# FFN activations of an encoder kernel kept in class order; the up products read them in token order

## The reference, cut to what matters

```python
h = rms_norm(x, ffn_pre_norm[l])
x = x + rms_norm(conv_gated_mlp(h, w_up[l], ffn_conv[l], w_down[l]), ffn_post_norm[l])

def conv_gated_mlp(h, w_up, conv_w, w_down):
    S = h.shape[1]
    u = h @ w_up                                   # 256 x 1024 by 1024 x 5632
    pad = CONV_WIDTH // 2
    up = jnp.pad(u, ((0, 0), (pad, pad), (0, 0)))
    u = sum(up[:, t:t + S] * conv_w[t] for t in range(CONV_WIDTH))
    gate, val = jnp.split(u, 2, axis=-1)
    return (jax.nn.gelu(gate, approximate=True) * val) @ w_down
```

## Time and profile before

| | |
|---|---|
| median of 3 runs | 1053.47 us (1053.18 to 1053.96) |
| the profiled execution | 1052.44 us |
| its span, first to last instruction | 1050.5 us |
| PE (matmuls) busy | 1026.9 us, 98% |
| PEld (weight loads) busy | 919.9 us, 88% |
| DVE busy | 657.0 us, 63% |
| ACT busy | 586.4 us, 56% |
| POOL busy | 127.0 us, 12% |
| mean granted clock of TensorE | 0.999 of full speed |
| read from HBM | 168.72 MB, 162 GB/s over the span |

### The profile page before, as it was taken

How to read it: one execution, slowest core, us unless ns; L and a number is a source line. 1 busy time by engine, 2 the same in 40 slices (tenths; PEclk the granted TensorE clock), 3 DMA queues, 4 the chain that set the end, 5 groups by cost and what they waited for, 6 DMA issues and landing times.

```text
span 1050.5 us, 15947 instructions
## 1 busy us (share of the span) xinstructions
PE 1026.9 (98%) x6325; PEld 919.9 (88%) x6325; DVE 657.0 (63%) x866; ACT 586.4 (56%) x843; POOL 127.0 (12%) x233
## 2 busy tenths in 40 slices
PE   7899999999999999999999999999999999999997
PEld 6789989888877999999898899998888789999996
DVE  4635566555585876767674345666555867676765
ACT  4567665555536554554475666665653466455452
POOL 3452133000000000000014421230000000000000
PEclk9999999999999999999999999999999999999999
DMA  8554445544434555555355543464345535555541
GB/s 233 176 169 141 123 149 164 178 161 160 141 130 171 169 186 207 179 182 201 119 180 173 150 142 120 130 222 160 122 154 179 167 128 175 200 193 168 201 160 41
DMA packets 106189, 170.79 MB, mean 163 GB/s; under 512 B 3345, under 2 KB 72772, under 8 KB 106116
## 3 DMA queue, kind: packets, MB, share of 16 engines
q1 hardware_dynamic: 104684, 166.36, 48.0%
q10 hardware_dynamic: 1352, 3.16, 0.9%
q0 software_dynamic: 80, 0.26, 0.2%
HBM read 168.72 MB, written 1.05 MB: 162 GB/s over the span
## 4 chain that ended last, share of the span: by engine, by line
PE 88%; DVE 5%; ACT 2%; DVEq 2%; DMA 1%; issue 1%; POOL 0%; POOLq 0%; ACTq 0%; SPq 0%
PE bank L1268 26%; PE bank L1270 26%; PE bank L1269 25%; PE bank L1558 2%; PE bank L1465 1%; PE bank L1486 1%; DVEq L1126 1%; PE bank L1551 1%; DVE hT_lo L996 1%; DVE merged L1127 1%; DVE w_lo L975 1%; PE bank L1474 1%; PE bank L1502 1%; DMA w_raw<-in_w_in_dram 1%; DMA par_rows<-in_attn_pre_norm_dram 1%
## 5 line engine op out<-in xcount | busy, mean ns | idle before, releaser
L975 DVE TENSOR_TENSOR w_lo<-w_raw,w_hi 128x2048 fp32r<-128x2048 f32 (+3 forms) x174 | 363.0, 2098 | 192.8 <-ACT w_hi L647 192.8
L647 ACT ACTIVATE w_hi<-w_raw 128x2048 fp32r<-128x2048 f32 (+3 forms) x174 | 302.4, 1752 | 52.3 <-PE bank L1270 46.7
L1268 PE MATMUL bank<-w_hi,hT_lo 128*128 128x512 f32 (+2 forms) x700 | 258.5, 369 | 2.8 <-DVE w_lo L975 2.7
L1270 PE MATMUL bank<-w_hi,hT_hi 128*128 128x512 f32 (+2 forms) x700 | 253.0, 361 | 0.0
L1269 PE MATMUL bank<-w_lo,hT_hi 128*128 128x512 f32 (+2 forms) x700 | 252.5, 361 | 0.0
L1268 PE MATMUL bank<-hT_hi,w_lo 128*128 128x256 f32 x704 | 199.9, 284 | 3.5 <-DVE hT_lo L996 3.2
L1269 PE MATMUL bank<-hT_lo,w_hi 128*128 128x256 f32 x704 | 199.2, 283 | 0.0
L1270 PE MATMUL bank<-hT_hi,w_hi 128*128 128x256 f32 x704 | 199.2, 283 | 0.0
L1268 PEld LDWEIGHTS bank<-w_hi,hT_lo 128*128 128x128 f32 x700 | 131.5, 188 | 19.3 <-DVE w_lo L975 3.8
L1270 PEld LDWEIGHTS bank<-w_hi,hT_hi 128*128 128x128 f32 x700 | 131.4, 188 | 14.1
L1269 PEld LDWEIGHTS bank<-w_lo,hT_hi 128*128 128x128 f32 x700 | 131.7, 188 | 13.1
(11 more groups left out here) (203 smaller groups left out, 1247.4 us busy)
## 6 DMA issues: line engine op xcount, KB each, us to landing
w_raw<-in_w_up_dram SPq DMA_DIRECT2D x44, 1024.0 KB, 4.9
w_raw<-in_w_in_dram SPq DMA_DIRECT2D x36, 1024.0 KB, 5.0
w_raw<-in_w_in_dram SPq DMA_DIRECT2D x36, 768.0 KB, 4.3
w_raw<-in_w_down_dram SPq DMA_DIRECT2D x22, 1024.0 KB, 5.4
w_raw<-in_w_out_dram SPq DMA_DIRECT2D x8, 1024.0 KB, 4.9
w_raw<-in_w_in_dram SPq DMA_DIRECT2D x8, 672.0 KB, 4.9
w_raw<-in_w_branch_mla_dram SPq DMA_DIRECT2D x4, 1024.0 KB, 4.8
w_raw<-in_w_branch_diff_dram SPq DMA_DIRECT2D x4, 1024.0 KB, 5.0
```

Of the source, the lines that this page charges most:

```text
L647: nc.scalar.activation(w_hi[:, n % RING, 0:nk * cols], raw[:, n % RING, 0:nk * cols], ACT.Copy).then_inc(hi_done, 1)
L975: V.tensor_tensor(w_lo[:, n % RING, s], raw[:, n % RING, s], w_hi[:, n % RING, s].bitcast(F32), ALU.subtract).then_inc(lo_done, 1)
L1268: PE.matmul(dst, lhs[1], rhs_hi, start=start, stop=False)
L1270: return PE.matmul(dst, lhs[0], rhs_hi, start=False, stop=stop)
```

## The change

The copies of the FFN turn no longer reorder: ACT and DVE write `hT_hi` and `hT_lo` contiguously, in class order, as in the other turns. The reordering goes into the read of the moving operand. A new view, `token_order`, walks place 64r + j with r innermost, so that the 256 columns come as 64 groups of 4 words, each word 64 words from the last. The PSUM view of the output is written with the same two dimensions but is contiguous, as before. The results in the banks, the convolution, `g` and the down products are the same. The number of instructions, all waits and all DMAs stay.

```diff
--- before.py
+++ after.py
@@ -449,13 +449,9 @@
             nk, cols = PIECES[n][3:5]
             return buf[:, n % RING, 0:nk * cols].rearrange("p (k n) -> p k n", k=nk)
 
-        def own_order(cols):
-
-            return cols.rearrange("p (j r) -> p r j", r=4)
-
-        def by_class(cols):
-
-            return cols.rearrange("p (r j) -> p r j", r=4)
+        def token_order(cols):
+
+            return cols.rearrange("p (r j) -> p j r", r=4)
 
         def own_order2(cols):
             return cols.rearrange("p (c j r) -> p c r j", c=2, r=4)
@@ -748,8 +744,6 @@
                         g0 = {"attn": PRE_A, "ffn": PRE_F, "latent": G_Q}[what]
                         for k in range(nk):
                             col, from_bank = dst[:, k0 + k, :], src[:, k * SEQ:(k + 1) * SEQ]
-                            if what == "ffn":
-                                col, from_bank = own_order(col), by_class(from_bank)
                             last = nc.scalar.activation(col, from_bank, ACT.Copy,
                                                         scale=par_all[:, l, g0 + k0 + k:g0 + k0 + k + 1])
                     last.then_inc(turn_hi, 1)
@@ -991,8 +985,6 @@
                         g0 = {"attn": PRE_A, "ffn": PRE_F, "latent": G_Q}[what]
                         for k in range(nk):
                             lo_k, hi_k, from_bank = lo[:, k0 + k, :], hi[:, k0 + k, :].bitcast(F32), src[:, k * SEQ:(k + 1) * SEQ]
-                            if what == "ffn":
-                                lo_k, hi_k, from_bank = own_order(lo_k), own_order(hi_k), by_class(from_bank)
                             last = V.scalar_tensor_tensor(out=lo_k, in0=from_bank, scalar=par_all[:, l, g0 + k0 + k:g0 + k0 + k + 1],
                                                           in1=hi_k, op0=ALU.mult, op1=ALU.subtract)
                     last.then_inc(turn_emptied, 1)
@@ -1342,9 +1334,9 @@
                         for k in range(8):
                             if j == 0:
                                 wait_turned(l, kind, c, k)
-                            last = passes(bank[4 + c % 4][:, j * SEQ:(j + 1) * SEQ],
+                            last = passes(bank[4 + c % 4][:, j * SEQ:(j + 1) * SEQ].rearrange("p (q r) -> p q r", r=4),
                                           (hi[:, k, j * P:(j + 1) * P], lo[:, k, j * P:(j + 1) * P]),
-                                          hT_hi[:, k, :], hT_lo[:, k, :], k == 0, k == 7)
+                                          token_order(hT_hi[:, k, :]), token_order(hT_lo[:, k, :]), k == 0, k == 7)
                     last.then_inc(piece_used, 1)
                     return
                 halves = 2 if cols == 1024 else 1
```

## The result

The changed kernel takes 1087.01 us (median of 4 runs, 1086.35 to 1088.54), the kernel before 1053.72 us beside it. The ratio is 1.0321, 95% interval 1.0306 to 1.0337: 33.3 us slower. The forecast was 1725 us with 1265 as the lower end. The sign was right, the size far out.

What follows compares the result with a forecast made beforehand. The prediction took PE, busy 98% of the span, as the bound: 675.8 us more for the up products' strided read, less 4.3 for the copies, on 1053.5 gave 1725 us. The range was 1265 to 1840 us, chance 0.82.

Steps and rivals of the forecast that it cites:

- PE as the bound, nothing added, everything else hidden: Whole kernel: PE busy 98% sets the time, no instruction is added, ACT's and DVE's work stays hidden behind PE.
- Parts 1 and 2, the copies: FFN turn: copies without stride end earlier, saving 3.9 us in two layers, or 4.3 us if products cost much more.
- the forecast 4.3 us: FFN turn, both layers: gain from unstrided copies if up products become much slower, 2.17 us a layer.
- Part 3, the read: Up products: each lone column costs 1.67 ns, so 0.440 us instead of 0.120 for 2112 matmuls, adding 675.8 us.
- X: Up products: new time from one product's start to the next, 0.120 us before, forecast 0.440.
- the first rival: Up products: a lone column costs two, 0.227 us per product, +221 us, 1274.5 us; chance 0.24.
- A gain below it is excluded: Up products: none can go below 0.120 us, already a column per cycle at the upper clock level.
- The page on memory lines: Up products: stride of 64 never hits a line twice in a row; two hits, counted in TensorE's columns, would give 1274.5 us.
- The price of a double: Up products: a lone column costs two, 0.227 us per product, 1274.5 us; chance 0.24.
- The case of no cost: Up products: the strided read costs PE nothing, only the copies' 3.9 us are gained, 1049.6 us; chance 0.15.
- The clock: PE: the granted clock might fall to 1.2 GHz, down products from 0.227 to about 0.440, +113, 1838 us; chance 0.05.
- theory L: Up products, from the follow-ups: fetching a 16-byte line not at hand costs; lines fetched a few columns ago are still there.

Runs made afterwards that it cites:

- e7_stride128: Against the changed kernel, up products read two streams 128 words apart in turn (0 128 1 129 ...); 1031.12 us.
- n5_two_streams_all: As n4_two_streams_copies, with weights of all 512-column products but the ukv ones also read in two streams 256 words apart; 1014.27 us, ratio 0.9629.
- n4_two_streams_copies: Against the kernel before, FFN copies put even tokens in one half, odd in the other; up products read the halves in turn; 1032.84 us, ratio 0.9808.
- e4_stride4: Against the changed kernel, up products read every fourth word, 64 in the innermost dimension, four times (0 4 8 ... 252 1 5 ...); 1287.29 us.
- e3_pairs: Against the changed kernel, up products read two adjacent words before each jump of 64 (0 1 64 65 128 129 ...); 1269.15 us.
- e2_read_alone: Against the kernel before, only the up products' read becomes that of the changed kernel, copies stay strided; 1090.25 us, ratio 1.0358.
- e11_no_reuse: Against the changed kernel, up products jump 64 words four times, then go on 4 words further into new lines (0 64 128 192 4 68 ...); 1325.19 us.
- e9_stride32: Against the changed kernel, up products jump by 32 words among eight lines (0 32 64 ... 224 1 33 ...); 1268.12 us.

## Why the prediction was wrong, step by step

- **PE as the bound, nothing added, everything else hidden: right.** PE is at 98%, and the sum of pitches and copies gives the span's difference.
- **Parts 1 and 2, the copies: right to a few hundredths in the trace.** DVE 0.87 us behind ACT, as forecast; eight copies in 3.23 us for 3.21; PE 0.86 us earlier; the forecast 4.3 us close the sum where PE is slow, and 3.6 us were measured alone for 3.9.
- **Part 3, the read: this step failed, twice.** The text said that two engines end at the same absolute time for an element that lies alone, that this "reads as a time of the memory", and that "a matmul that takes a new place for every column would see it too", so 0.440 us. First, the changed kernel's columns aren't at new places in the sense that counts. Its pattern comes back to the same four lines after four columns, and the runs show that such a return costs little: X = 0.1374. The stride of 64 words was taken as the property of the read, when it is the order of visits over the lines. Second, even words that are really alone cost 0.223 to 0.251 us and not 0.440: about double, as the first rival had it (0.227). Of all patterns tried none came near 0.440. The text itself called 1.67 ns the most that a group of four can take if reads don't overlap, and then used this bound as the price of a group; (0.223 - 0.013) / 256 and (0.251 - 0.013) / 256 make it 0.82 to 0.93 ns. That the change was slower, as forecast with 0.85, is in part luck: the loss comes from new lines in the same round, a cost that the text had no term for, and the step that was to cause it didn't happen.
- **"A gain below it is excluded": wrong too.** The text held that 0.120 us was as fast as 256 columns go. In e7_stride128 they take 0.1117.
- **The rows that misled.** L885 and L1232 agreed at 1.77 and 1.79 ns an element. In n5_two_streams_all the same two instructions, unchanged, are the groups

```profile
L901 ACT ACTIVATE g_hi<-conv_out 128x512 fp32r<-128x512 f32 x22 | 34.1, 1552 | 47.2 <-DVE conv_out L1246 47.2
```

```profile
L1248 DVE TENSOR_TENSOR g_lo<-conv_out,g_hi 128x512 fp32r<-128x512 f32 x22 | 30.1, 1370 | 35.6 <-ACT g_hi L901 35.6
```

  With 1115 and 1098 ns before, ACT's now costs 0.83 + (1552 - 634) / 512 = 2.62 ns an element and DVE's 1.00 + (1370 - 692) / 512 = 2.32. So their strided time depends on what PE reads beside them. One kernel shows it too: n4_two_streams_copies, ACT's timeline, once beside up products, read in two streams, and once beside down products, whose weights PE reads contiguously:

```profile
354.50 1.38 ACT L889 ACTIVATE g_hi<-conv_out 128x512 fp32r<-128x512 f32 x1 [0.76 <-DVE conv_out L1234]
...
446.10 1.11 ACT L889 ACTIVATE g_hi<-conv_out 128x512 fp32r<-128x512 f32 x1 [2.15 <-DVE conv_out L1234]
```

  It wasn't a constant of the memory, and the agreement of the two engines was no proof of one.
- **The page on memory lines.** The Trainium skill (Advanced Engine Details and Errata, "SBUF Cachelines") states that at least two hits on a 16-byte line are needed to absorb the access latency, and that another line at each access is penalised. This fits e4_stride4, where each line is hit once per visit and X is 0.2332. If two hits in a row were enough, as the prediction read it, e3_pairs should be free, and X is 0.2236; and a read that changes the line at each column should be double, where the changed kernel's X is 0.1374. In these runs the number of columns since the line was last used decides, and the measurements stand.
- **The rivals.** The price of a double was right for another pattern than this one. The case of no cost, given 0.15, was nearer than any other: 1049.6 us. No case stood between it and 1274.5, though its own test (0.002 us on X decides) showed that a small cost is enough to lose. The clock didn't fall.

## What to carry to other kernels

The cost of a moving operand's access pattern isn't in its stride alone: write down the sequence of words, mark the groups of four (fp32r) that they fall into, and see after how many columns each group is visited again. With a return within six columns a product of up to 256 columns took 0.112 to 0.140 us here, with a later one 0.223 to 0.251, against 0.120 contiguous. The first range isn't free where PE is the bound: 0.0175 us lost 33 us. Two interleaved streams are then worth a try even where the contiguous read seemed perfect: 0.0083 us per product of 256 columns and 0.0117 per product of 512, over 3960 products, together with about 2.7 us from the copies and less about 3 us of new waits, made 38.8 us here (1053.09 to 1014.27).

## What the runs showed of the hardware that was not expected

- **Two interleaved streams are faster than a contiguous read**: 0.1117 against 0.1200 us for 256 columns, 0.2161 against 0.2278 for 512. Why is open; that lines end at once or in turn makes no difference for two.
- **Four streams in step cost 0.1374, staggered by a word 0.1183**, and in step but only four words apart 0.1349.
- **The same instructions found two steady distances**: 0.1433 for the first 192 up products of layer 0, 0.1374 for nearly all others. In e2_read_alone it is layer 1 whose first 192 go at 0.1433, and layer 0 goes at 0.1374 from its start; in both kernels the longer distance ends with the first down products. What sets it off is open.
- **The dear patterns don't follow theory L's count of fetches.** e11_no_reuse is dearer (0.2508) than e4_stride4 (0.2332) and e9_stride32 (0.2229), though each column would fetch in all three; and e3_pairs, with half as many fetches, costs 0.2236 like e9_stride32. So theory L tells cheap patterns from dear ones, and doesn't give the price; lengths of jumps may matter among dear patterns, which no run separates.
- **ACT's and DVE's strided reads slow down with what PE reads beside them**: ACT's takes 1115 ns before, 1145 in n4_two_streams_copies, 1552 in n5_two_streams_all, where PE's waits for the low part behind it grew by 1.5 us. It isn't PE's pace that does it: in e11_no_reuse, the slowest kernel, DVE's takes 1251 ns instead of 1098. Their contiguous reads don't change (`split_hi` 1910 ns before, 1916 in n5_two_streams_all).
